# Gated delta rule and attention blocks on one core: the doubling products of the chunk inverse as 64x64 matmuls on the two diagonal quarters of the array

## The reference, cut to what matters

```python
def gated_deltanet(h, w_in, conv_w, a_log, dt_bias, o_norm_g, w_out):
    ...
    decay = jnp.exp(jnp.where(causal, G[..., :, None] - G[..., None, :], -jnp.inf))
    kk = jnp.einsum('bhcid,bhcjd->bhcij', kc, kc)
    tri = jnp.where(strict, bc[..., :, None] * kk * decay, 0.0) + jnp.eye(CHUNK, dtype=f32)
    rhs = jnp.concatenate([vc * bc[..., None], kc * (bc * jnp.exp(G))[..., None]], axis=-1)
    sol = lax.linalg.triangular_solve(tri, rhs, left_side=True, lower=True, unit_diagonal=True)
```

## Time and profile before

| what | value |
|---|---|
| median of 3 runs | 1408.72 us (1407.17 to 1408.93) |
| the profiled execution's own time | 1406.92 us |
| its span in the trace | 1405.1 us |
| PE busy | 1385.8 us (99% of the span) |
| DVE busy | 750.6 us (53%) |
| ACT busy | 595.3 us (42%) |
| mean granted TensorE clock | 0.998 of full |
| the eight heads' own steps in the trace | from 48.95 us to about 373 us |

### The profile page before, as it was taken

How to read it: one execution, slowest core, us unless ns; L and a number is a source line. 1 busy time by engine, 2 the same in 40 slices (tenths; PEclk the granted TensorE clock), 3 DMA queues, 4 the chain that set the end, 5 groups by cost and what they waited for, 6 DMA issues and landing times.

```text
span 1405.1 us, 18545 instructions
## 1 busy us (share of the span) xinstructions
PE 1385.8 (99%) x6729; PEld 1137.1 (81%) x6729; DVE 750.6 (53%) x1112; ACT 595.3 (42%) x930; POOL 0.2 (0%) x4
## 2 busy tenths in 40 slices
PE   7899999999999999999999999999999999999998
PEld 5788888888788888888887777778888888888886
DVE  6677777777474343343465444347543443434555
ACT  5565546545453133241445455463442332423342
POOL 0000000000000000000000000000000000000000
PEclk9999999999999999999999999999999999999999
DMA  4232222221243333333334221112433332233323
GB/s 154 88 76 47 61 72 60 60 75 45 73 126 105 92 91 103 90 103 104 90 90 150 75 61 45 49 56 75 150 105 105 90 106 89 90 104 90 97 82 105
DMA packets 42338, 124.09 MB, mean 88 GB/s; under 512 B 3952, under 2 KB 12720, under 8 KB 41776
## 3 DMA queue, kind: packets, MB, share of 16 engines
q1 hardware_dynamic: 33472, 117.08, 27.7%
q10 hardware_dynamic: 8816, 6.33, 2.3%
HBM read 119.17 MB, written 4.23 MB: 88 GB/s over the span
## 4 chain that ended last, share of the span: by engine, by line
PE 95%; DVE 2%; ACT 2%; DMA 1%; issue 1%; ACTq 0%; SPq 0%; DVEq 0%
PE acc L316 26%; PE acc L318 25%; PE acc L317 25%; PE ps L431 2%; PE ps L451 2%; PE ps L654 2%; PE ps L638 1%; PE ps L670 1%; DMA work<-rows 1%; PE ps L411 1%; DVE wl L292 1%; PE ps L316 0%; PE ps L682 0%; ACT wh L285 0%; PE ps L318 0%
## 5 line engine op out<-in xcount | busy, mean ns | idle before, releaser
L316 PE MATMUL acc<-xh,wh 128*128 128x512 f32 x1008 | 415.7, 412 | 9.3 <-DVE xl L1801 8.2
L318 PE MATMUL acc<-xh,wl 128*128 128x512 f32 x1008 | 394.4, 391 | 0.0
L317 PE MATMUL acc<-xl,wh 128*128 128x512 f32 x1008 | 393.6, 390 | 0.0
L285 ACT ACTIVATE wh<-raw 128x1024 fp32r<-128x1024 f32 x207 | 216.4, 1049 | 179.7 <-DMA raw<-in_weights 165.8
L292 DVE TENSOR_TENSOR wl<-raw,wh 128x1024 fp32r<-128x1024 f32 x207 | 252.7, 1221 | 72.5 <-ACT wh L285 69.9
L316 PE MATMUL acc<-yh,wh 128*128 128x512 f32 x608 | 237.9, 391 | 0.0
L318 PE MATMUL acc<-yh,wl 128*128 128x512 f32 x608 | 236.6, 389 | 0.0
L317 PE MATMUL acc<-yl,wh 128*128 128x512 f32 x608 | 236.5, 389 | 0.0
L316 PEld LDWEIGHTS acc<-xh,wh 128*128 128x128 f32 x1008 | 190.5, 189 | 49.0 <-DVE wl L292 9.5
L318 PEld LDWEIGHTS acc<-xh,wl 128*128 128x128 f32 x1008 | 189.6, 188 | 40.9
L317 PEld LDWEIGHTS acc<-xl,wh 128*128 128x128 f32 x1008 | 190.4, 189 | 37.4 <-issue 4.3
(11 more groups left out here) (243 smaller groups left out, 1206.7 us busy)
## 6 DMA issues: line engine op xcount, KB each, us to landing
raw<-in_weights SPq DMA_DIRECT2D x208, 512.0 KB, 3.5
work<-rows ACTq DMA_DIRECT2D x16, 256.0 KB, 7.0
h<-in_xT SPq DMA_DIRECT2D x4, 512.0 KB, 6.0
proj<-work ACTq DMA_DIRECT2D x2, 1024.0 KB, 4.2
work<-proj SPq DMA_DIRECT2D x2, 1024.0 KB, 7.3
outT<-h SPq DMA_DIRECT2D x8, 256.0 KB, 2.6
cst<-in_cst SPq DMA_DIRECT2D x1, 640.0 KB, 3.7
work<-in_pT SPq DMA_DIRECT2D x1, 512.0 KB, 5.2
```

Source lines behind the costliest of these rows:

```text
L285: nc.scalar.activation(slot(u)[0][:], raw[u.const % 2][:], ACT.Copy).then_inc(hi_done, 1)
L316: nc.tensor.matmul(dst[:], hi, mh[:, k, :], start=(n == 0), stop=False)
L317: nc.tensor.matmul(dst[:], hi, ml[:, k, :], start=False, stop=False)
L318: mm = nc.tensor.matmul(dst[:], lo, mh[:, k, :], start=False, stop=(n == KT - 1))
```

## The change

All products of levels 1 to 6 are written as matmuls of 64 rows by 64 columns. For levels 1 to 5 there are two a chunk where there was one: rows and columns 0 to 63, then rows and columns 64 to 127. `x(n)` moves 64 columns instead of 128; `tx(n)` moves the 32 packed columns that belong to its quarter (for n = 1 all 64, so that the other quarter's columns of `ps[1]` are written with zeros once). Both quarters write one bank, in different partitions. For level 6 the first chunk's products lose their extra half, which leaves four matmuls of 64x64 in one quarter; their number stays. The off-diagonal quarters of `ps[0]` keep what `kk` left there, which the mask makes zero. Ahead of every `x` and `tx` stands a semaphore instruction of PE (`small_tile`, 12 a head), which carries the wait for the operands and increments `level_begun`, for which nobody waits.

```diff
+            def small_tile():
+
+                pe.sem_inc(level_go, 1)
+
             def x(n):
                 def step():
                     pe.wait_ge(t_d, b * 6 + n)
+                    small_tile()
                     for c in range(C):
                         if n < 6:
-                            last = nc.tensor.matmul(ch(ps[0], c), ch(Lt, c), ch(Ti, c), start=True, stop=True)
+                            for lo in (0, HD):
+                                m = slice(lo, lo + HD)
+                                last = nc.tensor.matmul(ch(ps[0], c)[m, m], ch(Lt, c)[m, m], ch(Ti, c)[m, m],
+                                                        start=True, stop=True)
                         else:
-                            lo = HD if c else 0
-                            last = nc.tensor.matmul(ps[0][lo:, c * HD:(c + 1) * HD], ch(Lt, c)[0:HD, lo:],
+                            last = nc.tensor.matmul(ps[0][HD:, c * HD:(c + 1) * HD], ch(Lt, c)[0:HD, HD:],
                                                     ch(Ti, c)[0:HD, 0:HD], start=True, stop=True)
...
+                    small_tile()
                     for c in range(C):
                         if n < 6:
-                            last = nc.tensor.matmul(ps[1][:, c * HD:(c + 1) * HD], ch(TT0 if n == 1 else TT, c),
-                                                    Xs[:, c * HD:(c + 1) * HD], start=True, stop=True)
+                            for lo in (0, HD):
+                                m = slice(lo, lo + HD)
+                                to = slice(c * HD, (c + 1) * HD) if n == 1 else \
+                                    slice(c * HD + lo // 2, c * HD + lo // 2 + 32)
+                                last = nc.tensor.matmul(ps[1][m, to], ch(TT0 if n == 1 else TT, c)[m, m], Xs[m, to],
+                                                        start=True, stop=True)
                         else:
-                            m = HD if c else P
-                            last = nc.tensor.matmul(ps[2][0:m, c * HD:(c + 1) * HD], Xs[HD:, c * HD:c * HD + m],
+                            last = nc.tensor.matmul(ps[2][0:HD, c * HD:(c + 1) * HD], Xs[HD:, c * HD:(c + 1) * HD],
                                                     ch(TT, c)[HD:, HD:], start=True, stop=True)
```

More of the change, by code:

```diff
@@ L205, in build @@
                                                    sem("o_scaled"), sem("y_done"), sem("yh_done"), sem("yl_done"))
+        level_go = sem("level_begun")
         out_d = sem("out_stored")
```

## The result

The change takes 1399.37 us (median of 4 executions, 1397.25 to 1401.08), the kernel before on the same chip 1408.81 (1407.17 to 1408.93): ratio 0.9935, 95% interval 0.9918 to 0.9952. It is faster by 9.4 us where 12 were forecast.

The account below looks back on a forecast made before the run. The prediction took PE to be the bound, busy for 99% of the span. Its terms, -3.8 - 4.2 - 3.8 = -11.8, say -12 us, took 1408.7 to 1396.7 us; range 1391 to 1400 under full overlap, 1391 to 1410 wider.

Parts of the forecast that it names:

- What bounds it: Heads 2 to 7: PE is the bound, so time taken out of its queue is saved; 1.48 us a head.
- Full overlap of the quarters: Sixteen 64x64 passes, eight a quarter, run beside each other at 0.029 us a pass on the mean; chance 0.65.
- Rival 2's program order: Each quarter's pass starts no earlier than the one before it: +0.058 in 80 groups, 4.6 us, 1401 us; chance 0.07.
- x(1) to x(5) and tx(1): 48 groups in all, 1.28 us where 1.36 was: -0.08 each, -3.8 us.
- tx(2) to tx(5): 32 groups moving 32 columns, first and last pass each 0.027 shorter: 1.23 us, -0.13 each, -4.2 us.
- Level 6: x(6) and tx(6), 16 groups, one change of tile size less: 1.28 where 1.52 was, -3.8 us; needs no overlap.
- Semaphores: Twelve instructions a head: nothing in middle heads; where cover is gone, 0.05 us to wake and 0.05 for a load.
- Late next: DVE's L1356 after level 6 becomes late and PE waits at L465: at most 0.1 a head, +0.8 us.
- Heads 1 and 8: tx's operand waits in nine groups go away because x's result comes 0.2 us earlier: -0.7 us.
- The sum: All terms over eight heads: -11.8, say -12 us, giving a median of 1396.7 us.

Follow-up runs that it names:

- experiment 2: Against the change: at levels 1 to 5 each chunk's first quarter computed twice, 24 passes a group; 1430.99 us, ratio 1.0163 to the kernel before.
- experiment 3: Against the change: at levels 1 to 5 all four chunks' first quarters issued before the second quarters; 1417.26 us, ratio 1.0085 to the kernel before.
- experiment 5: Against the change: tx(2) to tx(5) move 64 columns instead of 32; 1398.13 us, ratio 0.9929 to the kernel before.
- experiment 1: Against the change: levels 1 to 5 again 128x128, only level 6 in 64x64; 1405.6 us, ratio 0.9983 to the kernel before.
- experiment 4: The kernel before, with its 128x128 products, plus the 12 semaphore instructions a head; 1408.48 us, ratio 1.0 to the kernel before.
- the second profile: Profile of the unedited change measured once more, in a second session of five executions; 1397.59 us, ratio 0.9922 to the kernel before.
- the last kernel of experiment 8: Against the change: 32x32 products at levels 1 to 4 in all heads, the unedited repeat; 1392.09 us, ratio 0.9886 to the kernel before.

## Why the prediction was right, and where it was off

- **What bounds it.** Right: heads 2 to 7 shrink by what the groups shrink.
- **Full overlap of the quarters.** Right, and the weightiest step. Sixteen passes start in 0.46 us; doubling one quarter adds 0.45 a group (experiment 2), so the passes of the second are free. Rival 2's program order is refuted too, by experiment 3, where the second quarter's first pass starts ahead of three that stand before it.
- **x(1) to x(5) and tx(1).** 0.08 forecast, 0.09 measured for x and 0.08 for tx(1): right.
- **tx(2) to tx(5).** The mis-sized term: "the first pass and the last are each shorter by half a product", 1.23. The first is (0.03, experiment 5), the last isn't: 1.25. Over 32 groups +0.8 us.
- **Level 6.** Right: 0.48 a head in two groups, also by itself (experiment 1), though there 0.12 of it goes into the stall of `w`.
- **Semaphores.** Right: nothing in the middle heads, and with the cover gone 0.06, within the "0.05 to wake, and 0.05 for a load" (experiment 4).
- **Late next.** The stall of at most 0.1 is real when level 6 is changed alone (0.12), but the shorter tx(5) removes it in the change: 0.02 at most where 0.1 a head stood.
- **Heads 1 and 8.** Where the sum failed beside tx. It gave them a full 1.48 each and 0.7 in waits that go away; they gave 0.85 and 1.15 in the second profile, together 0.96 under two full heads. The waits at tx(3) and tx(4) went as said (in head 8 such a group has 1.24 where it had 1.45), but others grew. PE and ACT in head 8 at level 6:

```profile
352.63 0.65 PE L467 MATMUL ps<-work 64*64 64x64 f32 x8 [0.62 <-ACT work L905]
...
351.02 1.06 ACT L286 ACTIVATE wh<-raw 128x1024 fp32r<-128x1024 f32 x1
352.11 0.38 ACT L905 ACTIVATE work<-ps 64x256 f32<-64x256 f32 x1
```

ACT's copy of x(6) waits behind its weight conversion, which begins no earlier against x(6) than before (351.02 - 350.44 = 0.58 us behind its first pass, 356.67 - 356.17 = 0.50 before); PE's 0.25 saved at x(6) turn into a wait of 0.62 at tx(6), where it was 0.20. Likewise the wait of the earlier trace rows for DVE's update at level 1 went from 0.20 to 0.48. In head 1 of the second profile the wait at tx(6) for ACT's copy is 0.6 too, where it was 0.2, that for DVE's conversion L293 is 1.2 (0.9 before), and that for the first inverse 3.1 (2.8 before).
- **The sum.** In the second profile, from head 1's first unit step: -0.85 - 8.36 - 1.15 = -10.4 us. The eight full heads of the forecast are -11.8: heads 2 to 7 lack 0.5 (tx less what x gives more), heads 1 and 8 lack 0.96. The median of the second session differs by 10.7, that of the first by 9.4. Two of the first session's four executions had a mean clock of 0.996, and the profiled one of them lost 2.55 us in head 1 with the longer spell; that this explains all of the difference of the medians wasn't shown, and the intervals of the two ratios overlap. The forecast of 1396.7 is the time of the fastest execution (1396.76); both medians lie in its range.

## What to carry to other kernels

Where PE is the bound, products that use only diagonal blocks are worth splitting into tiles: a group costs the passes of its fullest tile, plus an entry and an exit that were the same in every group of 64x64 behind big matmuls, here 0.33 and 0.15 us; write the matmuls with the tiles taking turns, since a tile whose eight passes come behind the other's eight is started four passes late. Count a saving head by head: where PE already waits for DVE or ACT, a shorter group only turns into a longer wait. Before a remainder of 2 or 3 us is explained by the change, run it again and look at the granted clock.

## What the runs showed of the hardware

- A pass of one 64x64 tile starts as soon as 0.01 us after that of the other, while passes in one tile keep 0.058; four 32x32 tiles start 32 passes within about 0.3 us.
- PE starts passes out of the program's order when they belong to different tiles: the first of the second quarter is the ninth in the program and started after five (experiment 3; read from the distances and from the length of its row, 0.27 where its neighbours have 0.22).
- The exit from a group of 64x64 to the big matmul is 0.15 us with 32 and with 64 columns moving, one stream or two. The change of tile size costs 0.10 on the way in (0.33 against 0.23). That agrees with the Trainium skill, "TensorEngine Tiling (Array Packing)", Tiling Modes, by which a change of mode drains the array.
- Granted clock at 1.2 GHz (0.50 in the rows) in head 1: a spell of 3.4 us in most of the profiles, of 10.2 or 10.3 us in two (the change's first, the last kernel of experiment 8), with 3.4 us in another execution of the same programs. In the change's first profile, ahead of it PE had waited 2.93 us for the first inverse of head 1:

```profile
51.06 0.68 PE L439 MATMUL ps<-work 64*64 64x64 f32 x16 [2.93 <-DVE work L1431]
```

That this wait is its cause was not shown.
